# Rows of V added by TensorE: one in sixteen instead of one in eight while cache pages are read

## The reference, cut to what matters

```python
def one_block(hb):                                   # 128 tokens
    qh = (hb @ wq).reshape(TOK_BLOCK, PEER_HEADS, D_KEY)
    ...                                              # top 16 of two key sets, per head
    ids = jnp.take_along_axis(cid, j, axis=-1)       # 8 heads x 16 experts a token
    g = jax.nn.softmax(top_s, axis=-1)
    act = jax.nn.gelu(jnp.einsum('thkd,td->thk', u_tab[ids], hb), approximate=False)
    return jnp.einsum('thk,thkd->td', g * act, v_tab[ids])

def one_seq(args):                                   # one sample sequence, 16 pages of 128 keys
    ...
    k = mla_keys(ckv_all, kpe_all, w_uk, g_k)
    sc = jnp.einsum('qhd,khd->hqk', qi, k) * scale
    p = jax.nn.softmax(sc, axis=-1)
    o_lat = jnp.einsum('hqk,kc->qhc', p, ckv_all)
```

## Time and profile before

| what | value |
|---|---|
| median of 3 runs | 2734.35 us (2725.26 to 2735.57) |
| the profiled execution | 2729.62 us |
| its span, first to last instruction | 2727.9 us |
| mean granted TensorE clock | 0.924 of full |
| busy over the span: PE, DVE, POOL, ACT | 86%, 77%, 53%, 34% |
| L2198 page keys on PE | 957.1 us in 3072 records |
| L2692 dot products on DVE | 622.8 us in 512 |
| L2592 additions on DVE | 577.4 us in 452 |
| L2214 expert rows on PE | 115.8 us in 224 records (56 rows) |
| L2099, L2106 gathers on POOL | 573.4 us and 663.7 us in 512 each |

### The profile page before, as it was taken

The page is one execution under the profiler, slowest core; times in us unless marked ns, Lnnn a source line. Parts: engine busy times, 40 slices in busy tenths (PEclk is TensorE's granted clock), DMA queues, the critical chain, the costliest instruction groups (busy, mean ns, idle before and its releaser), DMA issues.

```text
span 2727.9 us, 37121 instructions
## 1 busy us (share of the span) xinstructions
PE 2350.4 (86%) x11849; PEld 1633.3 (60%) x11849; DVE 2107.3 (77%) x4074; ACT 915.6 (34%) x3565; POOL 1448.7 (53%) x1212
## 2 busy tenths in 40 slices
PE   5999997997998987778999999999999989974343
PEld 3999996884447854345666666665666656642120
DVE  3674886995555327888998989898898979896797
ACT  3331102323242002223454444544454534430010
POOL 1122332212001104787777787787788767776575
PEclk7998998998999999889999999999999999996666
DMA  6335676455006768999999999999999999999997
GB/s 200 94 82 135 195 224 173 127 144 158 12 0 203 218 216 281 396 395 386 404 360 366 387 352 388 369 394 341 400 347 400 330 398 356 363 360 352 400 378 301
DMA packets 384720, 776.52 MB, mean 285 GB/s; under 512 B 49481, under 2 KB 199066, under 8 KB 384489
## 3 DMA queue, kind: packets, MB, share of 16 engines
q0 software_dynamic: 154736, 563.00, 54.7%
q1 hardware_dynamic: 208506, 186.51, 21.8%
q10 hardware_dynamic: 21284, 24.63, 3.0%
HBM read 744.85 MB, written 29.37 MB: 284 GB/s over the span
## 4 chain that ended last, share of the span: by engine, by line
PE 20%; issue 15%; DMA 13%; DVE 7%; POOL 6%; SPq 1%; ACT 1%; POOLq 0%; DVEq 0%; ACTq 0%
PE mix_pair L2198 14%; DMA mix_u<-in_peer_u,mix_ids 9%; POOL mix_v L2106 4%; DVE mix_acc L2592 3%; DVE mix_u L2692 3%; POOL mix_u L2099 2%; DMA pag_kpe<-in_cache_kpe 2%; PE mix_pair L2145 1%; PE mix_pair L2214 1%; PE mix_pair L2177 1%; DMA chs_keys<-in_peer_keys 1%; PE mix_pair L2201 1%; PE mix_pair L2233 1%; DMA keep_x<-mix_sc 1%; DMA mix_sc<-keep_ada 1%
## 5 line engine op out<-in xcount | busy, mean ns | idle before, releaser
L2198 PE MATMUL mix_pair<-pag_wx,pag_ckvT 128*128 128x384 f32 (+3 forms) x3072 | 957.1, 459 | 4.1 <-ACT mix_pair L2414 3.6
L2692 DVE CUSTOM_DVE_ANT_0 mix_u<-mix_u,mix_h 128x1024 f32<-128x1024 f32 x512 | 622.8, 1216 | 181.4 <-DMA mix_u<-in_peer_u,mix_ids 178.3
L2106 POOL DMA_INDIRECT mix_v<-in_peer_v,mix_ids x512 | 663.7, 1296 | 175.5 <-issue 164.3
L2198 PEld LDWEIGHTS mix_pair<-pag_wx,pag_ckvT 128*128 128x128 f32 x3072 | 563.5, 191 | 285.9 <-issue 17.1
L2099 POOL DMA_INDIRECT mix_u<-in_peer_u,mix_ids x512 | 573.4, 1120 | 272.5 <-issue 142.4
L2592 DVE SCALAR_TENSOR_TENSOR mix_acc<-mix_v,mix_coef,mix_acc 128x1024 f32<-128x1024 f32 x452 | 577.4, 1278 | 0.0
L2414 ACT ACTIVATE mix_pair<-mix_pair 128x128 f32<-128x128 f32 x1024 | 269.5, 263 | 351.3 <-PE mix_pair L2198 351.2
L386 POOL CAST inp_w_hi<-inp_w 128x1024 fp32r<-128x1024 f32 x73 | 112.2, 1537 | 377.3 <-DMA inp_w<-in_w_in 302.9
L2414 ACT ACTIVATION_READ_ACCUMULATOR mix_pair<-mix_pair 128x1 f32 x1024 | 191.2, 187 | 0.0
L386 POOL CAST mrg_w_hi<-mrg_w 128x1024 fp32r<-128x1024 f32 x24 | 28.5, 1186 | 306.2 <-DMA mrg_w<-in_w_br_a 271.9
L2214 PE MATMUL mix_pair<-mix_v,mix_diag 128*128 128x512 f32 x224 | 115.8, 642 | 60.1 <-ACT mix_diag L2431 58.3
(11 more groups left out here) (542 smaller groups left out, 4246.4 us busy)
## 6 DMA issues: line engine op xcount, KB each, us to landing
inp_w<-in_w_in SPq DMA_DIRECT2D x72, 512.0 KB, 4.2
pag_ckv<-in_cache_ckv SPq DMA_DIRECT2D x80, 256.0 KB, 15.6
mrg_w_ada<-in_w_ada SPq DMA_DIRECT2D x16, 1024.0 KB, 5.7
all_shared<-in_cache_ckv SPq DMA_DIRECT2D x48, 256.0 KB, 16.8
chs_wq<-in_peer_wq SPq DMA_DIRECT2D x11, 1024.0 KB, 17.0
keep_proj<-stp_out ACTq DMA_DIRECT2D x32, 260.0 KB, 2.9
ada_w_ada<-in_w_ada SPq DMA_DIRECT2D x4, 2048.0 KB, 10.0
stp_st<-in_state_ssm POOLq DMA_DIRECT2D x8, 1024.0 KB, 7.1
```

The lines of the kernel that those rows point to most:

```text
L2106: pool.indirect_dma_start(v[:, y % VR, :], None, v_rows, bass.IndirectOffsetOnAxis(at, 0)).then_inc(v_in[y % VR], 16)
L2198: last = pe.matmul(to, ckvT[:, g % 2, k, :], wx[:, k, lo:hi], start=(k == 0), stop=(k == KL - 1))
L2692: dve.tensor_tensor_reduce(u[:, r, :], u[:, r, :], h2[:, t % 2, :], 1.0, 0.0, ALU.mult, ALU.add, dots[:, t % 2, slot:slot + 1]).then_inc(u ...
```

## The change

One expression is edited, the rule for the rows of V that TensorE adds:

```diff
@@ -1958,7 +1958,7 @@
         TAIL = end[-1] + 20
         XEND = NSLOT + EXTRA + LAG + 8
-        by_pe = lambda x: x >= FIRST_PAGE and x % PE_EVERY == 3
+        by_pe = lambda x: x >= FIRST_PAGE and x % (PE_EVERY if x >= end[-1] else 2 * PE_EVERY) == 3
         on_pe = [x for x in range(NSLOT) if by_pe(x)]
         pe_index = {x: d for d, x in enumerate(on_pe)}
         last_on_pe = [max(x for x in on_pe if x // SL == t) for t in range(TT)]
```

## The result

The changed kernel takes 2738.7 us (median of 12 runs, 2728.93 to 2746.45), the kernel before 2728.6 us (12 runs, 2722.69 to 2737.68). The ratio is 1.0031, with a 95% interval of 1.0016 to 1.0047: some 8.5 us slower, inside the 0.5% that counts as no change and clear of zero. The forecast of 2737 us rested on +2.7 us. The median of three runs that it was put on (2734.35) was high: twelve runs give 2728.6. All ratios in this document leave out executions that took over 1.5% longer than the fastest of the same kernel.

A forecast was written before the change was run, and what follows sets the result against it. Two nearly equal streams, PE's pages and the POOL/DVE slot stream, were taken to bound the page stretch. Additions 10.8 less waits 8.1 gave +2.7 us on the 2734.35 median: 2737 us, range 2714 to 2757.

The forecast's parts named there:

- Even case: Page stretch: added additions nearly balance the waits that go, +2.7 us, 2737 us (2723 to 2749); chance 0.50.
- TensorE as the pace: Page stretch: PE's matmuls are the bound, so relief shows, 2706 us in full or 2720 by half; chance 0.26.
- every addition paid: DVE's slot stream pays for all 23 additions, 27.6 us: 2754 us, or 2762 without saved waits; chance 0.24.
- the additions on the path: DVE in full stretches: 9 of 23 added additions cost 1.20 us each, 10.8 us; bounds 0 to 27.6.
- The other 14 meet idle time: DVE outside full stretches: 14 added additions fit into waits for U and cost nothing; without cover 16.8 us more.
- Sharing by time: The 23 additions are split by the full stretches' share of time, 458 / 1176, giving 9 in full stretches.
- my nine full stretches: Nine parts of the page stretch, together 458 us, in which DVE is busy 98% and nothing hides an addition.
- one slot with a wait of 1.99 us: Slot behind the dot product at 1762.71: an addition of 1.20 us fits into DVE's wait for U, leaving 0.79.
- the rival in which a wait for U answers DVE's own release: Slot stream: a U buffer returned 1.20 us later brings its next row as much later; 2754 us, chance 0.24.
- Waits that go: DVE's waits behind PE and ACT: square root 6.4 us in full, half the exponentials' 3.4; gain 8.1, bounds 0 and 16.7.
- the clock: PE's granted clock could fall more often when idle; four more falls cost PE 6.8 us, forecast unchanged.
- The hold on POOL: Added additions could hold gathers by 0.9 us, 20.7 us for 23; costed at nothing since POOL keeps DVE's rhythm.

The follow-up runs named there:

- the second trace: Unchanged kernel before, traced once more on another chip like that of the result: slots 62 to 440 took 1179.2 us, against 1174.6 in its first trace.
- the last experiment: Kernel before with 23 one-input sums of 1024 elements added on VectorE, TensorE's rows all kept, against the kernel before: ratio 1.0042 (1.0021 to 1.0064), 11.5 us slower.

## Why the prediction was right, and which term was off

- **Even case, slightly slower.** The forecast was +2.7 us, the measurement +8.5 (4 to 13). The cases named as rivals for the fast chip, TensorE as the pace (2706 or 2720) and every addition paid (2754 or 2762), did not come. On one slow chip +1.42% was measured, at or above the second of them. That 2737 lies within 2 us of the measured 2738.7 is luck: the base was 5.7 us too high and the change 5.8 us too small.
- **The mis-sized term is the additions on the path, 9 x 1.20 = 10.8 us.** The step that failed is "The other 14 meet idle time: I cost them at nothing". Sharing by time was not the fault: 10 of the 23 additions fall into my nine full stretches. But outside them DVE doesn't wait in every slot, and I took one slot with a wait of 1.99 us for all. Counting at each place no more than 1.20 us, the waits there could cover 11.7 us (13.4 in the second trace), where I had 16.8. So 15.9 (14.2) us were on the path.
- **A term that I left out:** waits for U ahead of the other dot products grew by 5.6 us (7.1 against the second trace). Time that is gained at one place can be waited for at another. Why these waits grew is not shown; it is the direction of the rival in which a wait for U answers DVE's own release.
- **Waits that go, 8.1 us:** the idle time of DVE other than for U fell by 11.3 us (15.8). The size was too small, and its reason half wrong: the last experiment shows the same waits go with all rows on TensorE, because DVE comes later.
- The changed trace against the first of before: 27.6 us of additions, less 1.9 that DVE's other work took less, less 12.4 at the places, plus 5.6 ahead of other dot products, less 11.3 of other idle time, is +7.6 us, the growth of the stretch. Against the second trace the stretch grew by 3.0 us only. The 8.5 us rest on the runs, not on this sum.
- **TensorE, ACT, the clock:** PE's idle time rose from 27 to 59 us (I had said some 65) and turned in part into waits for DVE at the softmax, as said. PE's busy time fell by 25 us, not by 39.6: the page matmuls (L2198) took 963.7 us instead of 957.1, at a clock of 0.98 instead of 0.99, and the rest of the difference is not traced. PE had idle time for it.
- **The hold on POOL** at nothing was right in size, but not for the reason given: the added additions simply met gathers only at their very end, in 21 of 23 cases. All gathers together grew from 916 to 922 us.
- The signs that I had named for "slower" were mixed: waits for U fell below 110 us, to 103.8, but POOL's gathers passed 916.

What stays open: why the chips differ by 3 to 4%, why an addition costs nearly its whole time on the slow ones while VectorE has 180 us of idle time there, why waits for U grew elsewhere on the fast one, and what TensorE's relief alone gives there. No version tried beats the kernel before.

## What to carry to other kernels

When two streams of nearly equal length meet again and again, work moved from the one that the chain of waits names to the other costs there what no wait covers and frees only what the other one waited; so read that wait first (here 12 to 16 us of 1176) and take it as the bound on the gain. An average of idle time says little: look for the wait right behind each place at which a moved piece will stand, by the loop's own index. Trace the unchanged kernel twice before differences of a few microseconds between stretches are given a cause. Measure on more than one chip before a split tuned to 0.3% is believed.

## What the runs showed of the hardware

The same program took 2728 to 2733 us on two measurements and 2808 to 2840 us on three others, chip by chip. A gather instruction of POOL that starts while DVE runs an instruction with two SBUF inputs waits for the end of it, and then needs 0.81 us: 0.94 us alone, 1.20 with 0.39 us of an addition left, 1.86 with 1.05 us left; the one that met a sum with a single input, 0.40 us before its end, was not held (0.94). VectorE's 1024-element addition is recorded with 1.28 us, but the next instruction starts 1.20 us after it; the sum of 1024 elements is recorded with 1.21, and the next starts 1.13 after it.
